# The norm of a recurrence's output moved from a ones product to row sums and transposes, with VectorE's order changed

## The reference

```python
oc = hgrn2_chunkwise(c_q, kk, c_i, logf)                # (batch, tokens, 4 heads, 128)
oc = rmsnorm(oc, hgrn_norm_g[l].reshape(C_HEADS, C_VAL_DIM)).astype(x.dtype)
out_c = oc.reshape(b_, s_, C_WIDTH) * jax.nn.silu(c_gate)
...
def rmsnorm(x, g):
    x32 = x.astype(jnp.float32)
    y = x32 * lax.rsqrt(jnp.mean(x32 * x32, axis=-1, keepdims=True) + EPS)
    return y.astype(x.dtype) * g
```

## Time and profile before

| what | us |
|---|---|
| median of 3 runs | 1023.39 |
| lowest, highest | 1020.15, 1024.41 |
| the profiled execution's own time | 1023.19 |
| its span, from first to last instruction | 1021.4 |
| PE busy in it | 1000.9 |
| DVE busy | 625.8 |
| ACT busy | 503.5 |
| POOL busy | 285.1 |

### The profile page before, as it was taken

The page is one execution under the profiler, slowest core; times in us unless marked ns, Lnnn a source line. Parts: engine busy times, 40 slices in busy tenths (PEclk is TensorE's granted clock), DMA queues, the critical chain, the costliest instruction groups (busy, mean ns, idle before and its releaser), DMA issues.

```text
span 1021.4 us, 15835 instructions
## 1 busy us (share of the span) xinstructions
PE 1000.9 (98%) x6662; PEld 842.7 (83%) x6662; DVE 625.8 (61%) x856; ACT 503.5 (49%) x795; POOL 285.1 (28%) x144
## 2 busy tenths in 40 slices
PE   8989999999999999999999999999999999999997
PEld 7869899777888888888888989987788888888876
DVE  6878975788443544435628788477973434353652
ACT  6956675565452332223456766656455323232333
POOL 1212214432421423233212121153233222222430
PEclk9999999999999999999999999999999999999999
DMA  6512222122222323224342222222232232332602
GB/s 223 160 56 83 84 85 82 43 84 83 63 81 88 121 83 103 82 83 131 117 134 83 84 84 84 83 52 73 84 103 62 86 99 86 100 94 92 206 1 82
DMA packets 93430, 94.72 MB, mean 93 GB/s; under 512 B 2272, under 2 KB 91568, under 8 KB 93360
## 3 DMA queue, kind: packets, MB, share of 16 engines
q1 hardware_dynamic: 93232, 93.68, 29.6%
q10 hardware_dynamic: 128, 0.04, 0.0%
HBM read 91.62 MB, written 2.10 MB: 92 GB/s over the span
## 4 chain that ended last, share of the span: by engine, by line
PE 74%; DVE 14%; ACT 6%; issue 6%; DVEq 0%; POOL 0%; ACTq 0%; POOLq 0%
PE pj L529 22%; PE pj L530 22%; PE pj L531 22%; DVE w_lo L1314 2%; PE mx L529 1%; PE mx L530 1%; PE mx L531 1%; ACT w_hi L852 1%; DVE decay L1555 1%; DVE decay L1554 1%; ACT probs L981 1%; DVE decay_cum L1517 1%; DVE branch_out L1693 1%; PE mx L629 1%; DVE attnT L1579 1%
## 5 line engine op out<-in xcount | busy, mean ns | idle before, releaser
L1201 POOL TENSOR_TENSOR w_lo<-w_raw,w_hi 128x1024 fp32r<-128x1024 f32 (+1 forms) x89 | 195.6, 2198 | 566.2 <-ACT w_hi L852 566.2
L529 PE MATMUL pj<-h_hi,w_hi 128*128 128x512 f32 x832 | 330.5, 397 | 0.0
L530 PE MATMUL pj<-h_lo,w_hi 128*128 128x512 f32 x832 | 325.2, 391 | 0.0
L531 PE MATMUL pj<-h_hi,w_lo 128*128 128x512 f32 x832 | 325.1, 391 | 0.0
L852 ACT ACTIVATE w_hi<-w_raw 128x1024 fp32r<-128x1024 f32 (+1 forms) x179 | 159.0, 937 | 161.3 <-PE pj L531 161.3
L1314 DVE TENSOR_TENSOR w_lo<-w_raw,w_hi 128x1024 fp32r<-128x1024 f32 (+1 forms) x90 | 172.3, 1914 | 82.0 <-ACT w_hi L852 81.8
L529 PEld LDWEIGHTS pj<-h_hi,w_hi 128*128 128x128 f32 x832 | 157.0, 189 | 34.7 <-issue 3.0
L531 PEld LDWEIGHTS pj<-h_hi,w_lo 128*128 128x128 f32 x832 | 156.9, 189 | 33.2
L530 PEld LDWEIGHTS pj<-h_lo,w_hi 128*128 128x128 f32 x832 | 156.9, 189 | 32.1 <-issue 1.0
L1424 DVE TENSOR_TENSOR merge_gate<-pj,rstd 128x512 f32<-128x512 f32 x48 | 33.2, 691 | 168.1 <-PE pj L531 168.1
L970 ACT ACTIVATE merge_gate<-merge_gate,small 128x512 f32<-128x512 f32 x48 | 34.3, 715 | 83.9 <-DVE merge_gate L1424 83.9
(11 more groups left out here) (273 smaller groups left out, 1442.0 us busy)
## 6 DMA issues: line engine op xcount, KB each, us to landing
w_raw<-in_w_in SPq DMA_DIRECT2D x61, 1024.0 KB, 5.5
w_raw<-in_w_branch SPq DMA_DIRECT2D x24, 512.0 KB, 3.4
w_raw<-in_w_out SPq DMA_DIRECT2D x6, 1024.0 KB, 5.2
x_tokens<-in_x SPq DMA_DIRECT2D x4, 512.0 KB, 6.2
w_raw_last<-in_w_out SPq DMA_DIRECT2D x2, 1024.0 KB, 7.4
sp_w_rows<-in_sp_w SPq DMA_DIRECT2D x2, 512.0 KB, 5.6
out<-out_low SPq DMA_DIRECT2D x4, 256.0 KB, 2.0
out<-out_high SPq DMA_DIRECT2D x4, 256.0 KB, 2.3
```

Of the source, the lines that this page charges most:

```text
L529: pe.matmul(bank, wh, ah, start=first, stop=False)
L530: pe.matmul(bank, wh, al, start=False, stop=False)
L531: return pe.matmul(bank, wl, ah, start=False, stop=final)
L1201: return pool.tensor_tensor(out=dst, in0=full, in1=hi.bitcast(f32), op=ALU.subtract)
```

## The change

Four things are changed.

1. `recurrent_out` has its operands exchanged, so that a head's output comes out with 128 tokens on the partitions and its 128 values along the free axis, four such blocks in a bank.
2. ACT squares each block with `accum_out`, which gives a token's sum along its row (8 instructions of 128x128), and takes one Sqrt of the 128x8 sums. DVE takes the reciprocal of these and multiplies the PSUM blocks by it into `attnT`. PE transposes the eight blocks back (hooks 25 and 39), and a new DVE step `heads_taken` (phases 26 and 40) multiplies by the gain. The ones product, ACT's copy, Ln and Exp are gone.
3. In layer 0 `bounds` goes from phase 2 to the end of what phase 8 had before `normalise`; `split_lo(3)` goes from between rotations 0 and 1 to phase 4, after rotation 1.
4. In pair 1 the differences of levels 2 and 3 go behind the gate products of phase 28, and the operands of the last level go from phase 32 to phase 31 (`last_ops=31`).

```diff
-              first_taken=29, second_ops=30, last_exp=31, last_ops=32, second=32, second_taken=33, carry_exp=34,
+              first_taken=29, second_ops=30, last_exp=31, last_ops=31, second=32, second_taken=33, carry_exp=34,
...
                     if p == 1:
-                        pe.wait_ge(oc_rstd, upto(oc_rstd, 1))
+                        pe.wait_ge(oc_ready, upto(oc_ready, 1))
...
-                            last = pe.matmul(M[3 + hh][:, b], VC[:, tb, h * P:(h + 1) * P], AT[:, hh, b],
+                            last = pe.matmul(M[3 + hh][:, b], AT[:, hh, b], VC[:, tb, h * P:(h + 1) * P],
                                              start=True, stop=(tb == 0))
                             if tb > 0:
-                                last = pe.matmul(M[3 + hh][:, b], ST[:, hh, tb - 1, :], QC[p][:, hh, b],
+                                last = pe.matmul(M[3 + hh][:, b], QC[p][:, hh, b], ST[:, hh, tb - 1, :],
                                                  start=False, stop=True)
...
-                def head_norm(p):
-                    pe.wait_ge(oc_evac, upto(oc_evac, p + 1))
+                def transpose_heads(p):
+                    pe.wait_ge(oc_scaled, upto(oc_scaled, p + 1))
                     for hh in range(2):
-                        last = pe.matmul(M[3 + hh][:, :], ONE[:, :], AT[:, hh, :], start=True, stop=True)
-                    last.then_inc(ocn_done, 1)
-
+                        for tb in range(TB):
+                            b = slice(tb * P, (tb + 1) * P)
+                            last = pe.transpose(M[3 + hh][:, b], AT[:, hh, b], ID)
+                    last.then_inc(ocT_done, 1)
...
-                    for step, f in enumerate((transpose_khat, state_updates, recurrent_out, head_norm)):
+                    for step, f in ((0, transpose_khat), (1, state_updates), (2, recurrent_out), (4, transpose_heads)):
...
-                def recurrent_evac(p):
+                def head_squares(p):
+
                     act.wait_ge(oc_done, upto(oc_done, p + 1))
                     for hh in range(2):
-                        act.activation(OX[:, 2, 2 * p + hh, :], M[3 + hh][:, :], ACT.Copy)
-                        last = act.activation(AT[:, hh, :], M[3 + hh][:, :], ACT.Square)
-                    last.then_inc(oc_evac, 1)
-
-                def head_rstd(p):
-                    act.wait_ge(ocn_done, upto(ocn_done, p + 1))
-                    for hh in range(2):
-                        last = act.activation(AT[:, hh, :], M[3 + hh][:, :], ACT.Ln, bias=EP, scale=1.0 / P)
+                        for tb in range(TB):
+                            b = slice(tb * P, (tb + 1) * P)
+                            last = act.activation(AT[:, hh, b], M[3 + hh][:, b], ACT.Square,
+                                                  accum_out=HS[:, hh * TB + tb:hh * TB + tb + 1])
                     chained(last)
-                    act.activation(AT[:, :, :], AT[:, :, :], ACT.Exp, scale=-0.5).then_inc(oc_rstd, 1)
+                    act.activation(HR, HS, ACT.Sqrt, bias=EP, scale=1.0 / P).then_inc(oc_root, 1)
...
                 def head_scaled(p):
-                    dve.wait_ge(oc_rstd, upto(oc_rstd, p + 1))
+                    dve.wait_ge(oc_root, upto(oc_root, p + 1))
+                    chained(dve.reciprocal(HR, HR))
+                    for hh in range(2):
+                        last = dve.tensor_tensor(out=AT[:, hh, :].rearrange("p (b d) -> p b d", d=P),
+                                                 in0=M[3 + hh][:, :].rearrange("p (b d) -> p b d", d=P),
+                                                 in1=HR[:, hh * TB:(hh + 1) * TB].unsqueeze(2).to_broadcast([P, TB, P]),
+                                                 op=ALU.mult)
+                    last.then_inc(oc_scaled, 1)
+
+                def heads_taken(p):
+                    dve.wait_ge(ocT_done, upto(ocT_done, p + 1))
                     for hh in range(2):
                         h = 2 * p + hh
-                        last = dve.scalar_tensor_tensor(out=OX[:, 2, h, :], in0=OX[:, 2, h, :], scalar=hng[:, h:h + 1],
-                                                        in1=AT[:, hh, :], op0=ALU.mult, op1=ALU.mult)
+                        last = dve.tensor_scalar(OX[:, 2, h, :], M[3 + hh][:, :], hng[:, h:h + 1], None, ALU.mult)
                     last.then_inc(oc_ready, 1)
...
-                    phase[2].append((bounds,))
...
-                    if layer == 0 and r == 0:
-                        phase[n].append((split_lo, 3))
...
+                    if p == 0:
+                        for lev in (2, 3):
+                            phase[at_["first_ops"]].append((diffs, p, lev))
...
+                    phase[at_["khat"] + 5].append((heads_taken, p))
...
+                if layer == 0:
+                    phase[ATTN + 1].append((bounds,))
...
+                for lev in (2, 3):
+                    phase[STEPS[1]["first_ops"]].append((diffs, 1, lev))
```

More of the change, by code:

```diff
@@ L285, in build @@
         upd_done, state_ready, oc_done = lsem("upd_done"), lsem("state_ready"), lsem("oc_done")
-        oc_evac, ocn_done, oc_rstd, oc_ready = lsem("oc_evac"), lsem("ocn_done"), lsem("oc_rstd"), lsem("oc_ready")
+        oc_root, oc_scaled, ocT_done, oc_ready = (lsem(n) for n in ("oc_root", "oc_scaled", "ocT_done", "oc_ready"))
         wT_done, wT_evac, wT_ready = lsem("wT_done"), lsem("wT_evac"), lsem("wT_ready")
@@ L1820, in program @@
                     early = n <= FIRST[("cf", 0)] or n < NJ and JOBS[n][0] >= UNITS.index(("merge", 0)) - 1
-                    if 1 < v < LAST_OUT and v != 3 and early:
+                    if 1 < v < LAST_OUT and early:
                         split_lo(v)
@@ L1824, in program @@
                     for f, *a in phase[n]:
-                        if due and (f in (normalise, gate_product, diffs)
+                        if due and (f in (normalise, bounds, gate_product, diffs)
                                     or f is operands and n == STEPS[1]["second_ops"]):
```

8 lines of the change are left out of this document (3 added, 5 removed).

## The result

The changed kernel takes 1012.37 us in the median of 5 runs (1010.72 to 1013.89), the kernel before 1023.39 (1020.15 to 1024.41). The ratio of the two is 0.9894, with a 95% interval of 0.9879 to 0.9909: faster by 1.1%. The profiled execution took 1010.99 us, with a span of 1009.2.

A forecast was written before the change was run, and what follows sets the result against it. PE was taken as the bound, busy 1000.9 of 1021.4 us, so only less PE work or idle time could win: -3.4 + 1.0 - 2.8 - 3.3 - 1.7 - 3.5 = -13.7 from 1023.19 gives 1009.5 us, range 1005.0 to 1015.6.

The forecast's parts named there:

- PE's own work: Head norm, two pairs in two layers: eight transposes (0.87 us) replace a pair of ones products (1.72): 3.4 us less.
- The wait at the transposes: New head-norm transposes: PE waits 0 to 1.0 us for pair 0 of each layer if POOL holds DVE's reciprocal; 1.0 more in all.
- the 0.4 us of slack: Pair 0's transposes: DVE was to finish at 187.7 and PE to come at 188.1, so the step fits with 0.4 us to spare.
- The spatial step: Pair 1's gate product moves ahead of four differences, some 2.5 us earlier; the 1.4 us DVE wait goes in both layers: 2.8 less.
- what the head norm gave: Behind pair 0's norm: without Ln and Exp DVE no longer idles 4.85 us, and its following chain is 3 to 4 us earlier.
- The last level: Pair 1's recurrence products at L675: `key_blocks` moved forward, so the DVE waits go in both layers: 3.3 us less.
- slow clock in layer 0: The 5 us from 240, at 0.66 of full clock after the last level's 1.66 us wait, return to full: 1.7 us less.
- The rotations: Layer 0, before the scores: first query's rotation fills DVE's idle time; the 4.27 us wait and its slow clock go: 3.5 us less.
- The 0.7 us that I foresaw at job 6: Layer 0: the weight split behind the first rotation may come up to 0.7 us later, and job 6 would wait for it.
- the first rival: SBUF copy behind the rotations is held by POOL's split, so the rotations give 1.6 us, not 3.5: 1011.4 us, chance 0.27.
- only PE's work: Whole kernel: all waits come back at other places, as DVE's total is the same; only 3.4 us gained: 1019.8 us, chance 0.07.
- The waits of pair 1 stay: Spatial step and last level: DVE's work has not become less, so 2.8 + 3.3 + 1.7 us stay: 1017.3 us, chance 0.10.

The follow-up runs named there:

- The norm alone: Changed kernel with DVE's order (differences, last level's operands, `bounds`, `split_lo(3)`) put back as in the kernel before: 1016.15 us, ratio 0.9929 to the kernel before.
- the order alone: Kernel before with all the diff's moves in DVE's order and nothing of the norm's change: 1016.35 us, ratio 0.9932 to the kernel before.
- the cut version: Changed kernel with pair 1's burst of 192 thin products cut: levels 2 and 3 one job earlier, level 4 unmoved: 1008.36 us, ratio 0.9866 to the kernel before.
- 32 dead products: Changed kernel with 32 dead 1x1 products (128 instructions) ahead of PE's first job: 1015.27 us, ratio 0.9928 to the kernel before.

## Why the prediction was right, and where it was not

1009.5 us was forecast, 1012.37 measured, inside the range, and faster as said. The steps:

- **PE's own work**, 3.4 us less: 3.44.
- **The wait at the transposes**, 1.0 us more: none. The middle of 0 to 1.0 was taken, and it was the lower end in all four places. DVE ended at 180.52 + 1.29 = 181.81, ahead of PE's transposes at 182.16; the 0.4 us of slack held. That the reciprocal was not held was close: POOL's split began 0.03 us behind it, in both layers, and no run shows a reciprocal that comes under one. The row of 185.44, given for the rule that an operation reading PSUM is not held, is not under a split; `decay_cum<-pj` at 105.87 in the same trace is (0.68 us, under a split from 104.33 to 108.20), and so were the two scalings here.
- **The spatial step**, 2.8 us less: 2.97. The size was right and the cause half right. I named the four differences that the gate product overtakes and "what the head norm gave". The norm alone did it; the order alone would have too. Two causes for one wait add up to one wait.
- **The last level**, 3.3 us less and 1.7 of slow clock in layer 0: the wait for DVE went, 3.6 us. This is the step that failed: I took a removed wait as removed time. Behind it stood a wait for code that the DVE wait had hidden. Of the 5.0 us of this step 0.6 us are left (-3.60 -0.72 +3.74). I had asked what is late next only for DVE, POOL and ACT; the queue `q8 instruction` was on the page and I did not read it.
- **The rotations**, 3.5 us less: 4.03, by the way I described. The wait of 4.27 us and its slow clock went, and 0.88 us came back at the last level of pair 0. The 0.7 us that I foresaw at job 6 was 0.99. The copies were not held; the first rival had POOL within 0.1 us of the copy, and the second copy began 0.34 us before the split, so the forecast was right there by 0.34 us. Operations of one SBUF input can be held: `key_c<-key_c,small` took 2.59 us under a split (119.98 us, before) and 0.54 otherwise. But no run here has a copy between SBUF addresses that begins under a POOL split (the closest, with 32 dead products, overlaps its last 0.16 us and takes the usual 0.36), so whether the Trainium skill's rule on the shared port (page "SBUF — State Buffer", the section on the two separate sides) holds for copies as well stays open.
- **The sum**: -13.7 forecast; the runs' medians give -11.0. The wait that did not come at the transposes and the 0.5 us more at the rotations are 1.5 us in favour; the code waits and the clock behind the longest are 4.6 us against (0.71 + 1.91 + 0.28 + 1.7). So the nearness of 1009.5 to the 1012.37 is partly errors that cancel, and its nearness to the profiled execution's 1010.99 owes another 1.75 us to the start.
- **The rival "only PE's work"** said that all waits would come back at other places. Some did, through a resource that was not in its reckoning. **"The waits of pair 1 stay"** rested on DVE's work not having become less. DVE's work indeed rose (627.0 against 625.8 us), and the waits went all the same, since its idle time of 4.85 us was what counted.

The parts of the change are therefore worth, in their own terms: the norm about 7 us (1016.15), the other two moves nothing (1009.23 against 1008.36 in the cut version), and so what is left, 3.6 us by the ratios (0.9929 and 0.9894), the order at the rotations. The order alone gives 6.7 us against its own runs of the kernel before, the norm alone 6.9, and both together 11.0: they don't add.

The fastest versions are those with the burst in two pieces, 1008.3 us, 4 us under the changed kernel as timed on other chips; the intervals of the ratios (0.9852 to 0.9880 and 0.9879 to 0.9909) barely touch.

## What to carry to other kernels

Before counting a removed wait as time won, ask what was going on during it, and look at the queues that no line of the kernel issues to: here PE's code came in while PE waited for DVE. A long burst of very short instructions is where code can run out; here, cutting it in two with an ordinary job between cost nothing. And when a wait has two causes, take each away by itself before crediting either.

## What the runs showed of the hardware that was not expected

- PE can wait for its instructions. They come in packets of 16 KB, about 256 instructions; 28 waits of 0.17 to 3.66 us all ended at the same position within a packet, 1.20 to 1.55 us after the packet had landed. In these 28 cases the start of the packet lay 0.9 to 4.1 us behind the instruction that seems to ask for it. So where PE can run dry can be worked out in advance; whether it does, and for how long, only to within 1 to 2 us.
- 160 dead instructions at the start, 2.14 us of PE (most of which it stood idle there before), made the kernel 11 us slower (1023.38 against 1012.37), and 256 made it 0.5 us slower, which is within the scatter: the position in the packets is what differs.
- The same wait of PE can be followed by half clock or not. Of the 11 waits of 1.6 to 2.1 us in the middle of these profiles 6 were and 5 were not: granted clock 0.66 after 1.91 us in the changed kernel, 1.00 after 1.85 us of the same kind at the same instruction with the norm alone (its stretch below). The 7 longer ones, of 2.56 to 4.27 us, all were.

```profile
731.60:736.60 5.00, 4.96 (x22) 4.09 (x23) 4.60 (x14) 0.19 (x2) 0.73 (x1) 1.00 0.01 3
```
